# Attention with v stationary, two heads side by side, probabilities scaled on GpSimd before their transposes, and one ring of weight slots

## The chip, the cores and the metric

One core of a Trainium2 chip runs the kernel. The metric is device time in microseconds, the median of the runs. Inside a core five engines run at once and meet through semaphores: TensorE (PE; its weight loads are PEld), VectorE (DVE), ScalarE (ACT), GpSimd (POOL) and the queue of SyncE (SP), which issues DMAs.

## What is computed

One layer of a decoder trunk on 256 tokens of width 1024, 16 heads of 64. All is float32. With 256 tokens the block-sparse attention has only the causal block of its own:

```
y = rmsnorm(x, norm_mix)
q, k, v = split(y @ w_in, 3)              # 1024 x 3072
s = q @ k.T * 64**-0.5 + rel_bias[bucket(t - s)]   # causal, per head
h = x + (softmax(s) @ v) @ w_out          # 1024 x 1024
h = h + square(relu(rmsnorm(h, norm_mlp) @ w_up)) @ w_down   # 1024 x 4096, 4096 x 1024
out = rmsnorm(h, final_norm)
```

## The kernel before

Tokens lie in two blocks of 128 (`tb`). Every weight tile is 1 MB: 256 columns of an input matrix, or 256 rows of an output matrix. It lands in one of four slots of `raw`. ScalarE casts each half of it to a high part `w_hi` (`hi`, L490), VectorE subtracts it from `raw` to get a low part `w_lo` (`lo`, L668), and TensorE multiplies with both, so that three short products make one float32 product. Activations are split in the same way.

**Units.** A chunk `c` (of four) of attention is four heads: a tile of v, one of q, one of k. A v unit (L267 to L269) makes 128 tokens x 256 columns of v in 24 matmuls of 256 columns. A q or k unit (L287, L288) makes two heads' 128 features for all tokens in 8 matmuls of 512 columns and 8 of 256. Units write to banks 0 and 1 by turns. ScalarE takes out a part (`v_copy`, `qk_part`), VectorE the rest (`qk_sum`), and only then is the bank free.

**Attention of four heads `a`,** in two pairs `p`, heads `s` = 0 to 3:

- `scores` (L297, L299): per head a 128-column and a 256-column matmul over 64 rows; the two heads of a pair lie in the two halves of the array's rows. A float32 matmul is two passes, and two instructions in the profile.
- `add_bias` (VectorE, L740) adds the bias table and takes the row maximum; `softmax_exp` (ScalarE, L537) makes the exponentials in `probs` and their row sums.
- `probs_T` (L306): three transposes a head into the head's score bank; `pT_copy` (L747) brings them to `pT`.
- `values` (L320 to L322): `pT` is stationary, 64 columns of v stream: three matmuls a head, all into the bank `PV`.
- `sum_inverse` (L751) makes `rinv`, one over the row sums, and `out_rows_` (L756) multiplies the output rows by it.
- `out_T` (L330) transposes them, two a pair, and `out_hi` (L544), `out_lo` (L763) split them into `oT`.

**Order.** Each engine's order is written out by hand. In a loop over `c` = 1 to 3 TensorE puts the attention of chunk `c` - 1 between the units of chunk `c`:

```
scores(0) v(0) scores(1) v(1) probs_T(0) q(0) values(0) probs_T(1) q(1) values(1) out_T(0) k(0) out_T(1) k(1)
```

Behind the loop (L449 on) come the scores of the last four heads, the product with `w_out` in steps `mix(tb, k)` (L338), one pair's 128 features each, with the last attention between them, then the second norm (L249 transposes its rows) and the MLP in 16 steps. VectorE and ScalarE have lists of their own, in which the halves of weight tiles (`lo_in`, `hi_in`) stand between the attention steps. The q, k and v tiles use slots 0 to 2 and the fourth slot holds a `w_out` tile from the start; SyncE loads a tile as soon as `lo_done` says that the last one of its slot is converted. GpSimd only issues DMAs: the small tables, a bias table of 512 KB for each four heads (`tiles`, L225), and the gains of the norms.

Of the kernel before, what the change touches and what calls it, by code (L numbers as in the profile page):

```python
# [31 lines left out]
P = 128  # L32
# [17 lines left out]
UNITS = 6  # L50
# [25 lines left out]
def build(nc, x, rel_bias, norm_mix, norm_mlp, mlp_up, mlp_down, w_in, w_out, final_norm,  # L76
# [9 lines left out]
    with ExitStack() as ctx:  # L86
# [17 lines left out]
        v_sb = sb("v_sb", [P, TB, D])  # L104
# [3 lines left out]
        o_sb = sb("o_sb", [P, 2, TB, P])  # L108
# [24 lines left out]
        PV, OTB = 6, 7  # L133
# [13 lines left out]
        raw_free, scores_seen = sem("raw_free"), sem("scores_seen")  # L147
# [6 lines left out]
        scores_done, biased, exp_done = sem("scores_done"), sem("biased"), sem("exp_done")  # L154
        pt_done, pt_ready = sem("pt_done"), sem("pt_ready")
        rinv_done, pv_done, o_ready = sem("rinv_done"), sem("pv_done"), sem("o_ready")
        ot_done, othi_done, ot_ready = sem("ot_done"), sem("othi_done"), sem("ot_ready")
# [14 lines left out]

        @block.sync
        def _(sp):
            def load(slot, src, split):

                if split is not None:
                    sp.wait_ge(lo_done, split)
                    sp.sem_inc(raw_free, 1)
# [11 lines left out]
            load(1, w_in_v[:, :, 0:CW], None)  # L191
            load(2, w_in_v[:, :, D:D + CW], None)
            load(3, w_out_v[:, 6:8, :], None)
            with sp.Fori(1, CHUNKS_IN) as c:
                for slot, base in enumerate((2 * D, 0, D)):
                    load(slot, w_in_v[:, :, bass.ds(c * CW + base, CW)], 6 * c - 4 + 2 * slot)
            for q in range(3):
                load(q, w_out_v[:, 2 * q:2 * q + 2, :], 2 * (OUT0 + q - 3 + 1))
# [14 lines left out]
        def _(pool):  # L213
# [17 lines left out]
            with pool.Fori(1, CHUNKS_IN) as a:  # L231
                pool.wait_ge(biased, 4 * a)
                tiles(a)
# [5 lines left out]
        def _(pe):  # L239
# [13 lines left out]
            def v_unit(c, tb, first):  # L253

                if not first:
                    pe.wait_ge(lo_done, 6 * c + 2)
                    pe.wait_ge(qk_ready, 4 * c - 1 + tb)
                wh, wl = cols(w_hi, 0), cols(w_lo, 0)
# [13 lines left out]
            def qk_unit(c, u):  # L272

                slot = u // 2
                pe.wait_ge(lo_done, 6 * c + 2 * slot + 2)
                if u < 4:
                    pe.wait_ge(v_ready, 2 * c + u - 1)
                else:
                    pe.wait_ge(qk_ready, 4 * c + u - 3)
                feature_unit(bank[UNIT[u % 2]], slot, u % 2).then_inc(unit_done, 1)  # L280
# [11 lines left out]
            def scores(a, p):  # L292

                pe.wait_ge(qk_ready, 4 * a + 3 + p)
                heads = [(bank[SCORE[2 * p + h]], slice(h * DH, (h + 1) * DH)) for h in range(2)]
                for dst, dims in heads:
                    mm(dst[:, 0:P], qT[dims, p, P:T], kT[dims, p, 0:P], start=True, stop=True)  # L297
                for dst, dims in heads:
                    mm(dst[:, P:3 * P], qT[dims, p, 0:P], kT[dims, p, :], start=True, stop=True  # L299
                       ).then_inc(scores_done, 1)  # L300

            def probs_T(a, p):
                for h in range(2):
                    pe.wait_ge(exp_done, 4 * a + 2 * p + h + 1)
                    for b in range(3):
                        last = nc.tensor.transpose(bank[SCORE[2 * p + h]][:, b * P:(b + 1) * P],  # L306
                                                   probs[:, 2 * p + h, b * P:(b + 1) * P], ident[:])
                    last.then_inc(pt_done, 1)

            def values(a, p):  # L310

                if p == 1:
# [606 lines left out]
```

## Time and profile before

| | |
|---|---|
| runs | 324.13, 324.78, 325.31 us |
| median | 324.78 us |
| profiled execution, first to last instruction | 323.0 us |
| TensorE busy | 309.5 us, 96% |
| VectorE busy | 205.7 us, 64% |
| ScalarE busy | 160.9 us, 50% |
| GpSimd busy | 6.5 us, 2% |

The profiled execution has no time of its own beside its span; the median of the runs is 1.8 us above that span, which is what lies around the first and last instruction. Busy times of TensorE overlap, since its matmuls are pipelined, so what a step costs is read from one start to the next. The loop runs from 32.86 to 103.16 us, three turns of 23.43 or 23.44 us; the MLP's steps run from 142 to 317 us.

### The profile page before, as it was taken

How to read it: one execution, taken by the hardware profiler on the slowest of the kernel's cores; microseconds unless marked ns; L12 is line 12 of the kernel's file. 1: busy time of each engine (PE TensorE's matmuls, PEld its weight loads, DVE VectorE, ACT ScalarE, POOL GpSimd, SP SyncE). 2: the span in 40 equal slices, each digit the busy share in tenths (PEclk: the TensorE clock that was granted, in tenths of full speed). 3: DMA queues.
4: the chain of work that ended last, by engine and by line, in shares of the span. 5: the costliest groups of instructions: out<-in, count | busy, mean ns of one | idle time of the engine just before them, and what ended most of it. 6: DMA issues, size and time to landing. Idle time of an engine off the chain costs nothing.

```text
span 323.0 us, 5025 instructions
## 1 busy us (share of the span) xinstructions
PE 309.5 (96%) x1734; PEld 261.9 (81%) x1734; DVE 205.7 (64%) x366; ACT 160.9 (50%) x293; POOL 6.5 (2%) x14
## 2 busy tenths in 40 slices
PE   5699999999999999989999999999999999999992
PEld 2588898998997888988888888888888888888881
DVE  3786665665756657968755854675485567548454
ACT  2684734834833836535643544464455446434322
POOL 2001000000000000000000000000000000000000
PEclk9999999999999999999999999999999999999999
DMA  6989764463454373554756557465745656430003
GB/s 204 363 300 336 254 195 130 130 195 131 152 185 125 124 260 90 185 169 145 223 166 205 187 148 242 153 214 152 222 167 162 228 165 223 132 130 0 0 2 130
DMA packets 36589, 55.90 MB, mean 173 GB/s; under 512 B 1073, under 2 KB 29905, under 8 KB 36578
## 3 DMA queue, kind: packets, MB, share of 16 engines
q1 hardware_dynamic: 35586, 52.50, 49.9%
q0 software_dynamic: 992, 3.25, 3.6%
q8 instruction: 7, 0.11, 0.2%
q14 instruction: 4, 0.03, 0.0%
HBM read 54.67 MB, written 1.07 MB: 173 GB/s over the span
## 4 chain that ended last, share of the span: by engine, by line
PE 89%; DVE 4%; ACT 3%; DMA 2%; issue 1%; SPq 0%; DVEq 0%; ACTq 0%
PE bank L338 32%; PE bank L287 27%; PE bank L288 14%; PE bank L267 3%; PE bank L268 2%; PE bank L269 2%; DMA raw<-in_a_w_in_dram 2%; DVE w_lo L668 2%; PE bank L376 1%; PE bank L306 1%; PE bank L377 1%; PE bank L321 1%; PE bank L322 1%; PE bank L299 1%; PE bank L320 1%; PE bank L297 1%
## 5 line engine op out<-in xcount | busy, mean ns | idle before, releaser
L668 DVE TENSOR_TENSOR w_lo<-raw,w_hi 128x1024 fp32r<-128x1024 f32 x96 | 115.6, 1222 | 64.9 <-ACT w_hi L490 61.8
L287 PE MATMUL bank<-yT,w_hi 128*128 128x512 f32 x368 | 131.6, 399 | 0.0
L490 ACT CAST w_hi<-raw 128x1024 fp32r<-128x1024 f32 x95 | 97.6, 1048 | 56.0 <-PE bank L338 55.1
L288 PE MATMUL bank<-yT,w_lo 128*128 128x256 f32 x368 | 103.3, 281 | 0.0
L287 PEld LDWEIGHTS bank<-yT,w_hi 128*128 128x128 f32 x368 | 69.1, 188 | 16.7 <-DVE w_lo L668 0.6
L338 PE MATMUL bank<-w_hi,hT 128*128 128x512 f32 x256 | 73.3, 396 | 0.0
L288 PEld LDWEIGHTS bank<-yT,w_lo 128*128 128x128 f32 x368 | 69.5, 189 | 0.6
L338 PEld LDWEIGHTS bank<-w_hi,hT 128*128 128x128 f32 x256 | 47.1, 188 | 11.0
L338 PE MATMUL bank<-w_lo,hT 128*128 128x512 f32 x128 | 41.0, 397 | 0.0
L338 PEld LDWEIGHTS bank<-w_lo,hT 128*128 128x128 f32 x128 | 24.1, 188 | 5.9
L528 ACT ACTIVATE part<-bank 128x256 f32<-128x256 f32 x16 | 6.2, 385 | 33.0 <-PE bank L288 33.0
L551 ACT COPY part<-bank 128x256 f32<-128x256 f32 x30 | 11.2, 372 | 22.9 <-PE bank L288 22.9
L267 PE MATMUL bank<-w_hi,yT 128*128 128x256 f32 x64 | 19.5, 305 | 2.7 <-DVE yT L720 2.3
L338 PE MATMUL bank<-w_hi,oT 128*128 128x512 f32 x64 | 19.3, 399 | 0.0
L268 PE MATMUL bank<-w_lo,yT 128*128 128x256 f32 x64 | 18.6, 291 | 0.0
L269 PE MATMUL bank<-w_hi,yT 128*128 128x256 f32 x64 | 18.6, 291 | 0.0
L537 ACT ACTIVATE probs<-probs,negmax 128x128 f32<-128x128 f32 (+1 forms) x32 | 14.2, 445 | 6.1 <-DVE negmax L740 6.1
L557 ACT CAST hT<-s_sb 128x256 fp32r<-128x256 f32 x32 | 13.0, 407 | 8.2 <-DVE s_sb L782 8.2
L267 PEld LDWEIGHTS bank<-w_hi,yT 128*128 128x128 f32 x64 | 12.7, 198 | 5.4 <-DVE yT L720 2.7
L777 DVE TENSOR_TENSOR z_sb<-bank,part 128x256 f32<-128x256 f32 x30 | 12.6, 421 | 4.2 <-ACT part L551 4.2
L787 DVE TENSOR_TENSOR hT<-s_sb,hT 128x256 fp32r<-128x256 f32 x32 | 13.4, 419 | 1.9 <-ACT hT L557 1.9
L782 DVE SCALAR_TENSOR_TENSOR s_sb<-z_sb 128x256 f32<-128x256 f32 x32 | 13.6, 425 | 1.1
(73 smaller groups left out, 261.3 us busy)
## 6 DMA issues: line engine op xcount, KB each, us to landing
raw<-in_mlp_up_dram SPq DMA_DIRECT2D x16, 1024.0 KB, 5.5
raw<-in_mlp_down_dram SPq DMA_DIRECT2D x16, 1024.0 KB, 4.7
raw<-in_a_w_in_dram SPq DMA_DIRECT2D x11, 1024.0 KB, 6.7
raw<-in_a_w_out_dram SPq DMA_DIRECT2D x4, 1024.0 KB, 5.7
bias_sb<-bias_by_distance POOLq DMA_DIRECT2D x4, 512.0 KB, 5.2
h_sb<-in_x_dram SPq DMA_DIRECT2D x2, 512.0 KB, 5.2
raw<-in_a_w_in_dram SPq DMA_DIRECT2D x2, 512.0 KB, 7.2
out_dram<-y_sb SPq DMA_DIRECT2D x4, 256.0 KB, 2.2
```

What stands on the lines that cost most here:

```text
L267: mm(acc, yT[:, k, HI, tok], wh[:, k, :], start=(k == 0), stop=False)
L268: mm(acc, yT[:, k, HI, tok], wl[:, k, :], start=False, stop=False)
L269: last = mm(acc, yT[:, k, LO, tok], wh[:, k, :], start=False, stop=(k == KB - 1))
L287: mm(dst[:], wh[:, k, own], yT[:, k, :, :], start=(k == 0), stop=False, skip_group_check=True)
L288: last = mm(dst[:, 0:T], wl[:, k, own], yT[:, k, HI, :], start=False, stop=(k == KB - 1), skip_group_check=True)
L338: last = mm(bank[ACC[tb][c]][:], lhs(l), w[:, r, c * 512:(c + 1) * 512], start=first, stop=(stop and l == LO))
L490: nc.scalar.copy(w_hi[:, slot, part_of], raw[:, slot, part_of]).then_inc(hi_done, 1)
L537: last = nc.scalar.activation(probs[:, s, own], probs[:, s, own], ACT.Exp, bias=negmax[:, p, 2 * tb + h:2 * tb + h + 1], scale=-1.0, accum ...
L557: nc.scalar.copy(hT[:, par, i, HI, :], s_sb[:, i, :]).then_inc(hhi_done, 1)
L668: v.tensor_tensor(w_lo[:, slot, own], raw[:, slot, own], f32(w_hi[:, slot, own]), ALU.subtract).then_inc(lo_done, 1)
L782: v.scalar_tensor_tensor(s_sb[:, i, :], z_sb[:, i, :], 0.0, z_sb[:, i, :], ALU.max, ALU.mult).then_inc(s_done, 1)
L787: v.tensor_tensor(hT[:, par, i, LO, :], s_sb[:, i, :], f32(hT[:, par, i, HI, :]), ALU.subtract).then_inc(hT_ready, 1)
```

## The change

**TensorE.** `values` now has v stationary and streams `pT`: per head a matmul of 256 columns with the first token block's v and one of 128 columns with the second's. The output comes out as 64 features x tokens, the second head of a pair in partitions 64 to 127 of the same bank (`VALUES[p]`), which is the layout of `oT`. So `out_T`, `out_rows_` and `o_sb` go. The order of key blocks in `pT` is reversed (`(2 - b) * P`). All four heads' values are one block, and so are all four heads' scores.

**Scaling.** `probs` is multiplied by `rinv` on GpSimd (`normalise`), two instructions a head, before `probs_T`, which now waits for `normed` instead of `exp_done`.

**Order.** The units of a chunk come as q, k, v. `scores(c)` stands at the end of turn `c`; that of chunk 0 stands behind the first q unit of turn 1. Behind the loop three mixes of the second token block, not two, come before `mix_last(0)`.

**Weights.** Tiles are numbered through (`IN_PARTS`, then four of `w_out`) and use slot `t % 4`. A turn converts tiles 3c + 3 to 3c + 5; tile 5 is converted ahead of the loop and only one `w_out` tile behind it, not two. Loops over `c` are unrolled, and `v_sb` holds one chunk.

```diff
+IN_PARTS = [(0, "v"), (0, "q"), (0, "k")] + [(c, part) for c in range(1, CHUNKS_IN) for part in "qkv"]
...
-        PV, OTB = 6, 7
+        VALUES = [6, 7]
...
+            for t, (c, part) in enumerate(IN_PARTS):
+                if t:
+                    own = slice(PART_BASE[part] + c * CW, PART_BASE[part] + (c + 1) * CW)
+                    load(t % SLOTS, w_in_v[:, :, own], 2 * (t - SLOTS) + 2 if t >= SLOTS else None)
+            for q in range(CHUNKS_OUT):
+                load(q, w_out_v[:, 2 * q:2 * q + 2, :], 2 * (OUT0 + q - SLOTS) + 2)
...
+            def normalise(a, s):
+
+                p, h = s // 2, s % 2
+                pool.wait_ge(rinv_done, 2 * a + p + 1)
+                for tb, own in ((0, slice(0, P)), (1, slice(P, 3 * P))):
+                    last = nc.gpsimd.tensor_scalar(probs[:, s, own], probs[:, s, own],
+                                                   rinv[:, p, 2 * tb + h:2 * tb + h + 1], None, ALU.mult)
+                last.then_inc(normed, 1)
+
+            for a in range(CHUNKS_IN):
+                for s in range(4):
+                    normalise(a, s)
+                if a + 1 < CHUNKS_IN:
+                    pool.wait_ge(biased, 4 * a + 4)
+                    tiles(a + 1)
...
-                    pe.wait_ge(exp_done, 4 * a + 2 * p + h + 1)
+                    pe.wait_ge(normed, 4 * a + 2 * p + h + 1)
...
+            def values(a):
+
+                pe.wait_ge(v_ready, 2 * a + 2)
+                if a:
+                    pe.wait_ge(ot_ready, 2 * a)
+                for p in range(2):
+                    pe.wait_ge(pt_ready, 4 * a + 2 * p + 2)
+                    heads = [(bank[VALUES[p]][h * DH:(h + 1) * DH, :], 2 * p + h,
+                              slice((2 * p + h) * DH, (2 * p + h + 1) * DH)) for h in range(2)]
+                    for dst, s, own in heads:
+                        mm(dst[:, 0:T], v_sb[:, 0, own], pT[:, s, P:3 * P], start=True, stop=False)
+                    for dst, s, own in heads:
+                        last = mm(dst[:, 0:P], v_sb[:, 1, own], pT[:, s, 0:P], start=False, stop=True)
+                    last.then_inc(pv_done, 1)
...
+            for c in range(1, CHUNKS_IN):
+                a = c - 1
+                qk_unit(c, "q", 0)
+                if c == 1:
+                    scores(0)
+                qk_unit(c, "q", 1)
+                probs_T(a, 0)
+                qk_unit(c, "k", 0)
+                probs_T(a, 1)
+                qk_unit(c, "k", 1)
+                values(a)
+                v_unit(c, 0)
+                v_unit(c, 1)
+                scores(c)
...
             for k in range(4):
                 mix(0, k)
             probs_T(a, 0)
+            mix(0, 4)
             probs_T(a, 1)
-            mix(0, 4)
-            values(a, 0)
             mix(0, 5)
-            values(a, 1)
-            out_T(a, 0)
+            pe.wait_ge(pt_ready, 4 * a + 2)
             mix(1, 0)
-            out_T(a, 1)
+            values(a)
             mix(1, 1)
+            mix(1, 2)
             mix_last(0)
-            for k in range(2, PAIRS - 2):
+            for k in range(3, PAIRS - 2):
                 mix(1, k)
...
+            for c in range(1, CHUNKS_IN):
+                a, t = c - 1, 3 * c + 3
                 softmax_exp(a, 0)
                 softmax_exp(a, 1)
+                hi_tile(t, 0)
+                qk_part(c, "q", 0)
                 softmax_exp(a, 2)
                 softmax_exp(a, 3)
+                hi_tile(t, 1)
+                qk_part(c, "q", 1)
...
                 add_bias(a, 0)
                 add_bias(a, 1)
+                lo_tile(t, 0)
                 sum_inverse(a, 0)
                 add_bias(a, 2)
                 add_bias(a, 3)
+                qk_sum(c, "q", 0)
+                lo_tile(t, 1)
+                sum_inverse(a, 1)
+                qk_sum(c, "q", 1)
                 pT_copy(a, 0)
                 pT_copy(a, 1)
+                lo_tile(t + 1, 0)
```

On TensorE, the values of a pair and what follows them in the loop, before:

```order
L320 MATMUL bank<-v_sb,pT 128x64
L321 MATMUL bank<-v_sb,pT 128x64
L322 ISA
L322 MATMUL bank<-v_sb,pT 128x64
L320 ISA
L320 MATMUL bank<-v_sb,pT 128x64
L321 MATMUL bank<-v_sb,pT 128x64
L322 ISA
L322 MATMUL bank<-v_sb,pT 128x64
L330 MATMUL bank<-ident,o_sb 128x128 x2
```

and now, both pairs, with the end of the k unit ahead and the v unit's first matmuls behind:

```order
L310 MATMUL bank<-yT,w_lo 128x256
L344 MATMUL bank<-pT,v_sb 64x256 x2
L346 MATMUL bank<-pT,v_sb 64x128 x2
L344 MATMUL bank<-pT,v_sb 64x256 x2
L346 MATMUL bank<-pT,v_sb 64x128 x2
L292 MATMUL bank<-w_hi,yT 128x256
L293 MATMUL bank<-w_lo,yT 128x256
```

Six matmuls a pair have become four, of 64 output partitions, and the transposes of `o_sb` are gone.

On VectorE, from behind the last bias of four heads to the copies of the second pair's transposes, in the loop now (L679 is `lo`, L761 `sum_inverse`, L740 `qk_sum`, L757 `pT_copy`):

```order
L740 SCALAR_TENSOR_TENSOR qT<-bank,part 128x256 [waits part_done]
L679 TENSOR_TENSOR w_lo<-raw,w_hi 128x1024 [waits hi_done]
L761 RECIPROCAL rinv<-rowsum 128x4 [waits exp_done]
L740 SCALAR_TENSOR_TENSOR qT<-bank,part 128x256 [waits part_done]
L757 COPY pT<-bank 128x384 [waits pt_done] x2
L679 TENSOR_TENSOR w_lo<-raw,w_hi 128x1024 [waits hi_done]
L740 SCALAR_TENSOR_TENSOR kT<-bank,part 128x256 [waits part_done]
L757 COPY pT<-bank 128x384 [waits pt_done] x2
```

The second `sum_inverse` stands behind a weight conversion, as before; what is new is that the second pair's transposes wait for it.

On GpSimd, which computed nothing before, between the DMA of a gain and that of the next bias table (L237 is `normalise`):

```order
L229 DMA gain<-in_norm_mlp_dram 128x1024 [waits y_done]
L237 ISA
L237 TENSOR_SCALAR probs<-probs,rinv 128x128 [waits rinv_done]
L237 TENSOR_SCALAR probs<-probs,rinv 128x256
L237 TENSOR_SCALAR probs<-probs,rinv 128x128 [waits rinv_done]
L237 TENSOR_SCALAR probs<-probs,rinv 128x256
```

Eight such instructions now stand ahead of each bias table's DMA.

## Rows read from the trace of the kernel before

**Rows 1.** The page: the span, and TensorE's busy time, share and instructions.

```profile
span 323.0 us, 5025 instructions
...
PE 309.5 (96%) x1734; PEld 261.9 (81%) x1734; DVE 205.7 (64%) x366; ACT 160.9 (50%) x293; POOL 6.5 (2%) x14
```

**Rows 2.** The page: the chain that ended last, shares by engine.

```profile
PE 89%; DVE 4%; ACT 3%; DMA 2%; issue 1%; SPq 0%; DVEq 0%; ACTq 0%
```

**Rows 3.** Timeline of TensorE, second turn: start us, length us, what, count.

```profile
56.22 0.49 PE L297 MATMUL bank<-kT,qT 64*128 64x128 f32 x4
...
57.08 0.39 PE L267 MATMUL bank<-w_hi,yT 128*128 128x256 f32 x1
...
60.15 0.49 PE L297 MATMUL bank<-kT,qT 64*128 64x128 f32 x4
...
63.98 0.82 PE L306 MATMUL bank<-ident,probs 128*128 128x128 f32 x6
64.55 0.48 PE L287 MATMUL bank<-yT,w_hi 128*128 128x512 f32 x1
...
67.46 0.33 PE L320 MATMUL bank<-v_sb,pT 128*128 x2
...
68.74 0.83 PE L306 MATMUL bank<-ident,probs 128*128 128x128 f32 x6
...
73.47 0.39 PE L330 MATMUL bank<-ident,o_sb 128*128 128x128 f32 x2
73.61 0.48 PE L287 MATMUL bank<-yT,w_hi 128*128 128x512 f32 x1
...
79.66 0.49 PE L297 MATMUL bank<-kT,qT 64*128 64x128 f32 x4
```

**Rows 4.** 0.02 us windows of L299 alone: length, busy and instructions in flight.

```profile
56.54:56.56 0.02, 0.01 (x2) 0.02 (x4) 1.00 0.00 0
...
56.76:56.78 0.02, 0.02 (x4) 0.00 (x0) 1.00 0.00 0
```

**Rows 5.** Timeline of TensorE behind the loop, to the norm's transposes.

```profile
104.95 0.74 PE L338 MATMUL bank<-w_hi,oT 128*128 128x512 f32 x2
...
107.35 1.07 PE L338 MATMUL bank<-w_hi,oT 128*128 128x512 f32 x4
...
108.71 1.07 PE L338 MATMUL bank<-w_hi,oT 128*128 128x512 f32 x4
...
129.44 1.03 PE L249 MATMUL bank<-ident,y_sb 128*128 128x128 f32 x8
```

**Rows 6.** Timeline of VectorE: the scaling of the norm's first rows.

```profile
127.92 0.88 DVE L703 TENSOR_SCALAR y_sb<-y_sb,stat 128x512 f32<-128x512 f32 x2
```

**Rows 7.** Timelines of ScalarE (three rows) and VectorE behind the loop.

```profile
104.87 0.40 ACT L537 ACTIVATE probs<-probs,negmax 128x128 f32<-128x128 f32 x1 [1.29 <-DVE negmax L740]
...
105.76 1.03 ACT L490 CAST w_hi<-raw 128x1024 fp32r<-128x1024 f32 x1
106.70 0.40 ACT L537 ACTIVATE probs<-probs,negmax 128x128 f32<-128x128 f32 x1
...
104.19 0.29 DVE L740 CUSTOM_DVE_ANT_0 probs<-bank,bias_sb 128x128 f32<-128x128 f32 x1 [0.15 <-PE bank L299]
...
106.83 1.23 DVE L668 TENSOR_TENSOR w_lo<-raw,w_hi 128x1024 fp32r<-128x1024 f32 x1 [1.44 <-ACT w_hi L490]
107.97 0.17 DVE L751 RECIPROCAL rinv<-rowsum 128x4 f32<-128x4 f32 x1
```

**Rows 8.** Groups of VectorE's instructions by shape: busy us, mean ns, idle before.

```profile
L747 DVE COPY pT<-bank 128x384 f32<-128x384 f32 x16 | 8.0, 549 | 2.2 <-PE bank L306 2.2
...
L740 DVE CUSTOM_DVE_ANT_0 probs<-bank,bias_sb 128x256 f32<-128x256 f32 x16 | 6.7, 420 | 0.0
...
L740 DVE CUSTOM_DVE_ANT_0 probs<-bank,bias_sb 128x128 f32<-128x128 f32 x16 | 4.6, 287 | 4.4 <-PE bank L299 2.8 <-DMA bias_sb<-bias_by_distance 1.5
...
L703 DVE TENSOR_SCALAR y_sb<-y_sb,stat 128x512 f32<-128x512 f32 x8 | 3.5, 485 | 0.4
```

More of the change, by code:

```diff
@@ L290, in feature_unit, with scores @@
                 return last
[L292 to L300, printed above, removed]
+            def scores(a):
+                for p in range(2):
+                    pe.wait_ge(qk_ready, 4 * a + 3 + p)
+                    heads = [(bank[SCORE[2 * p + h]], slice(h * DH, (h + 1) * DH)) for h in range(2)]
+                    for dst, dims in heads:
+                        mm(dst[:, 0:P], qT[dims, p, P:T], kT[dims, p, 0:P], start=True, stop=True)
+                    for dst, dims in heads:
+                        mm(dst[:, P:3 * P], qT[dims, p, 0:P], kT[dims, p, :], start=True, stop=True
+                           ).then_inc(scores_done, 1)
@@ L419, in _ @@
             mm(bank[BIAS][0:HEADS, 0:BV], rel_sb[:], onehot_sb[:], start=True, stop=True).then_inc(bias_summed, 1)
-            for u in range(2, UNITS):
-                qk_unit(0, u)
-            with pe.Fori(1, CHUNKS_IN) as c:
-                scores(c - 1, 0)
-                v_unit(c, 0, False)
-                scores(c - 1, 1)
-                v_unit(c, 1, False)
-                probs_T(c - 1, 0)
-                qk_unit(c, 2)
-                values(c - 1, 0)
-                probs_T(c - 1, 1)
-                qk_unit(c, 3)
-                values(c - 1, 1)
-                out_T(c - 1, 0)
-                qk_unit(c, 4)
-                out_T(c - 1, 1)
-                qk_unit(c, 5)
+            for part in "qk":
+                for i in range(2):
+                    qk_unit(0, part, i)
+            for c in range(1, CHUNKS_IN):
[12 more added lines that the diff above has]
+                scores(c)
             a = CHUNKS_IN - 1
-            scores(a, 0)
-            scores(a, 1)
+            pe.wait_ge(v_ready, TB * CHUNKS_IN)
             for k in range(4):
@@ L622, in _ @@
             softmax_exp(a, 3)
+            hi_tile(OUT0 + 3, 1)
             nc.scalar.preload_act_table(ACT.Sqrt)
-            for half in range(2):
-                hi(3, half, 16)
             out_hi(a, 0)
@@ L814, in _ @@
                                    ).then_inc(bias_vec, 1)
-            lo_in(0, 2, 1)
-            lo_in(1, 0, 0)
-            qk_sum(0, 2)
-            lo_in(1, 0, 1)
-            qk_sum(0, 3)
-            lo_in(1, 1, 0)
-            qk_sum(0, 4)
-            lo_in(1, 1, 1)
-            qk_sum(0, 5)
-            with dve.Fori(1, CHUNKS_IN) as c:
-                a = c - 1
+            lo_tile(2, 1)
+            lo_tile(3, 0)
+            qk_sum(0, "q", 0)
+            lo_tile(3, 1)
+            qk_sum(0, "q", 1)
+            lo_tile(4, 0)
+            qk_sum(0, "k", 0)
+            lo_tile(4, 1)
+            qk_sum(0, "k", 1)
+            lo_tile(5, 0)
+            lo_tile(5, 1)
+            for c in range(1, CHUNKS_IN):
+                a, t = c - 1, 3 * c + 3
                 add_bias(a, 0)
                 add_bias(a, 1)
-                lo_in(c, 2, 0)
+                lo_tile(t, 0)
                 sum_inverse(a, 0)
```

215 lines of the change are left out of this document (84 added, 131 removed).

## The prediction

> **What bounds the kernel now.** I read the page's busy shares first: TensorE is busy for 309.5 of 323.0 us [rows 1]. The chain that ended last says the same from the other side: 89% of it is TensorE, 4% VectorE, 3% ScalarE [rows 2]. So an edit counts by what it takes off TensorE's queue or adds as a wait in it; work on VectorE, ScalarE and GpSimd costs nothing until TensorE waits for it. Next I read one turn of the loop in TensorE's timeline [rows 3]: 56.22 to 79.66, 23.44 us without a hole. The reader should look at start times there, since durations overlap: a score pair takes 57.08 - 56.22 = 0.86 us, a v unit 3.07, a transposition of two heads 0.57, a q or k unit 2.91, the values of two heads 1.28, a transposition of o 0.14. Inside a v unit 24 matmuls stand 0.12 apart (2.88); the other 0.19 is the change of array shape to and from the 64-row scores. Of a q unit 0.09 is a slower first start behind a transpose, so 2.82 inside.
>
> **What is removed from TensorE.** The new values of a pair are two matmuls of 256 and two of 128 columns, each in two passes, with the heads in two halves of the array. That is the form of a score pair, whose heads lie in two halves of the rows: two 256-column instructions are in flight at 56.55, and two more come at 56.76 [rows 4]. So side by side works there, and a step is set by the turn-round of some 0.2 us, not by columns. The trace has no column halves; bounds are 1.28 (no gain) and about 0.6 (if 64-column weights load faster than the 128-column ones). I take the score pair's 0.86, the nearest form. Per turn of the loop:
> - values: 2 x 1.28 = 2.56 becomes 2 x 0.86 + 0.19 for the shape = 1.91; saves 0.65.
> - the two transpositions of o go: 0.14 + 0.14 and the 0.09 behind the second; 0.37.
> - four score heads in one block: one change of shape less, 0.19; one slower start less, 0.09.
> That is 1.3 a turn, 3.9 for three. Behind the loop, from 104.95 to the norm's transposes at 129.44, lie 24.49 us, of which 14 mix steps of 1.36 are 19.04 [rows 5]. The rest, 5.45, is transposes, values and what TensorE waited between them. It becomes 2 x 0.66 + 1.91 = 3.23; saves 2.2. **Removed: 6.1 us.** The norm's scaling ends at 128.80 [rows 6] while its transposes begin at 129.44; they would now be due 1.36 sooner, 128.08. But the conversions that stood ahead of that norm come a step earlier too, and only its own chain from the last mix is left, so I cost this at 0, at most 0.7.
>
> The merged ring moves two halves of weight conversion (0.94 on ScalarE, 1.14 on VectorE each [rows 7]) from behind the loop to ahead of it. Their cover is the four units of the first chunk, 11.3 us; if that were short, the first biases would slip by up to 2.3. The bias table load now stands behind four scalings on GpSimd, with half a turn to spare. Unrolled loops only mean more code to fetch. All this I cost at 0.
>
> **What is added: a wait for the scaled probabilities.** Before, 1/sum was applied to the output rows and was nobody's cover. Now GpSimd multiplies the probabilities, and only then may TensorE transpose them. The queue order matters more than the multiplication, since the second 1/sum stands on VectorE behind a conversion that waits for ScalarE. Let T0 be the end of the four scores; behind the loop the trace shows that arrangement with T0 = 104.95. From it and the steps of [rows 7] (a head's exponentials 0.89, a ScalarE conversion 0.94 to the next operation and 1.03 to its end, a VectorE conversion 1.14):
> - bias of head 0 at T0 - 0.76, exponentials 0 and 1 from -0.08 to 1.70, conversion to 2.73, VectorE's part 2.77 to 3.91, first 1/sum there.
> - bias of head 2 at 4.0, exponentials 2 and 3 from 4.68 to 6.46 (0.68 behind it, as 104.87 is behind 104.19), conversion to 7.49, VectorE's part 7.53 to 8.67, second 1/sum to 8.84.
> - GpSimd starts heads 2 and 3 at about 8.95 and needs G for each. With a hand-over of 0.1, three transposes (half of 0.57) and a slower start, k unit 1 begins at 9.4 + 2G.
> By its own work TensorE would be there at 2.92 + 2.82 + 0.57 + 2.91 + 0.57 = 9.8 in turns 2 and 3. In turn 1 the scores stand behind the first q unit, which leaves one unit less of cover: 7.0. So the waits are 2.4 + 2G in turn 1 and 2G - 0.4 in each of the others, **1.6 + 6G** in all. Queued behind that wait are k unit 1, the values, v, and the next scores, so TensorE loses all of it. The first pair (scaled by about 4.2 + 2G, due at 5.7) costs nothing of its own up to G = 0.75. Behind the loop four mixes, 5.4 us, and a fifth before the second pair cover the chain: 0.
>
> G is the number that this trace lacks: GpSimd computes nothing here. Its work is an instruction of 128x128 and one of 128x256. VectorE's 512-column multiplication by a column of scalars takes 485 ns, which scaled to 384 columns is 0.36, the lower bound; its bias operation has just these two shapes, 287 + 420 = 0.71 [rows 8]; twice that, 1.42, is the upper bound. I take 0.71, the row of the same shapes. **Added: 1.6 + 4.3 = 5.9 us. Sum: -6.1 + 5.9 = -0.2**; the two balance at G = 0.75. The profile spans 323.0 us, so 322.8; the runs' median of 324.78 stands 1.8 above the span, so 324.6. A change within 0.3% (1.0 us) can't be told from none.
>
> The rows give only VectorE as a likeness. The Trainium skill (GPSIMD Engine Reference, "Performance versus the Vector engine") calls GpSimd the wrong choice for ordinary elementwise work, about twice slower than VectorE; that speaks against this change, and taken at G = 1.42 would make the sum +4.0. The same section states 1.03 cycles an element at 1.2 GHz for light one-input bodies; an estimate from that page is 0.33 us and two dispatches, and would make the sum about -1.8. No row here shows either.
>
> **The rivals.**
> 1. GpSimd is quick, G about 0.4, or the column halves turn round faster than the row halves. At G = 0.36 the wait is 3.8 and the sum -2.3: 322.5; with values of 0.6 a pair (8 x 0.26 less) 320.4. For it: one input, dense rows. Against it: 485 ns for 512 columns is VectorE's fastest row, 420 ns for 256 its usual one. Chance 0.31.
> 2. GpSimd is slow: the wait takes the place of what was saved. Place: the second transposition of each turn. It decides from G = 0.75 and passes 1 us at G = 0.92; at 1.42 the wait is 10.1, the sum +4.0: 328.8. For it: GpSimd's shortest time for anything is unknown here. Against it: the shapes are small. Chance 0.17.
> 3. VectorE and GpSimd keep each other out. Behind the second 1/sum VectorE has an addition and two copies of 549 ns each [rows 8], then at about 10.0 a conversion with two SBUF inputs. Head 3's wide multiplication would start at 8.95 + 0.71 + 0.29 = 9.95. If the conversion is first, the multiplication waits for its end at 11.15, 1.2 later, three times: +3.6 - 0.2 = +3.4, 328.2. The converse order costs TensorE nothing. Chance 0.11, since it needs both the exclusion and the loss of a close race.
> This is what the Trainium skill (SBUF — State Buffer, "SBUF: two separate sides") would have: GpSimd and a VectorE operation with two SBUF inputs share a port pair, held by whoever starts first for a whole instruction. No run of the kernel before can show it.
> 4. The change doesn't do what it says: heads in column halves run one after the other at 0.2 a pass, 1.7 a pair and not 0.86. 8 x 0.84 = +6.7: 331.3. Against it: [rows 4]. Chance 0.04.
>
> **How the numbers follow.** My forecast, G between 0.6 and 0.9 with nothing kept out, has 0.37: 324.6, itself from 323.9 to 325.7. It is nearly all within 0.3%, but some of it combines with a quicker or slower pair: 0.29 same, 0.05 faster, 0.03 slower. Rival 1 adds 0.31 to faster, rivals 2 to 4 add 0.32 to slower; 0.36, 0.29, 0.35. The range leaves out rival 4 and the ends of 1 and 2: 321.0 to 328.6.
>
> **What would show it.** Right: the transposes of the second pair start some 0.1 us behind GpSimd's end, TensorE idle about 3.8 us in turn 1 and 1.0 in turns 2 and 3, all of it ahead of the probabilities' transposes; turns of 23.1 us and a first one some 3 us longer; values at 0.86 a pair; no new wait behind the loop. Wrong: GpSimd's starts more than 1.0 apart per head or lying behind VectorE's conversions (rivals 2, 3), less than 0.5 (rival 1), the four passes of a shape one after another (rival 4), or TensorE waiting at a q or v unit, which my chain has nowhere.

## The result and the profile after

The changed kernel takes **332.32 us**, the median of 4 runs (330.91 to 332.93), against 324.95 of the kernel before on the same chip: a ratio of 1.0225 [1.0197, 1.0252]. It is slower by 7.4 us, outside my range, where I had forecast no change. The profiled execution took 332.65 us, its span is 330.8: 7.8 more than that of [rows 1].

The page of the changed kernel, its first part, the granted clock, the chain's shares and three groups:

```profile
span 330.8 us, 4655 instructions
...
PE 308.2 (93%) x1686; PEld 256.8 (78%) x1686; DVE 201.4 (61%) x358; ACT 160.0 (48%) x293; POOL 33.9 (10%) x46
...
PEclk9999969999999999999999999999999999999999
...
PE 80%; DVE 5%; POOL 5%; ACT 5%; DMA 2%; issue 1%; SPq 0%; DVEq 0%; ACTq 0%
...
L330 PE MATMUL bank<-ident,probs 128*128 128x128 f32 x48 | 8.8, 298 | 10.5 <-POOL probs L237 10.2
```

TensorE has 48 matmuls less and is hardly less busy; its share of the chain fell from 89% [rows 2] to 80%. What took its place is GpSimd (5%), and ScalarE and VectorE in front of it. The last row names the place: the transposes of the probabilities (L330) wait 10.2 us, in the whole program, for the multiplications of L237. I had added 5.9.

The timeline of TensorE in the second turn, which answers to [rows 3]; in brackets what ended an idle time before the row:

```profile
61.43 0.49 PE L320 MATMUL bank<-kT,qT 64*128 64x128 f32 x4
...
62.19 0.39 PE L320 MATMUL bank<-kT,qT 64*128 64x128 f32 x4
62.41 0.60 PE L322 MATMUL bank<-kT,qT 64*128 64x256 f32 x4
62.94 0.50 PE L309 MATMUL bank<-yT,w_hi 128*128 128x512 f32 x1
...
68.99 0.55 PE L330 MATMUL bank<-ident,probs 128*128 128x128 f32 x3
70.47 0.55 PE L330 MATMUL bank<-ident,probs 128*128 128x128 f32 x3 [0.93 <-POOL probs L237]
...
75.83 0.55 PE L330 MATMUL bank<-ident,probs 128*128 128x128 f32 x3 [1.59 <-POOL probs L237]
76.13 0.48 PE L309 MATMUL bank<-yT,w_hi 128*128 128x512 f32 x1
...
79.13 0.65 PE L344 MATMUL bank<-pT,v_sb 128*64 128x256 f32 x4
79.61 0.39 PE L346 MATMUL bank<-pT,v_sb 128*64 128x128 f32 x4
79.83 0.60 PE L344 MATMUL bank<-pT,v_sb 128*64 128x256 f32 x4
80.26 0.39 PE L346 MATMUL bank<-pT,v_sb 128*64 128x128 f32 x4
80.58 0.39 PE L292 MATMUL bank<-w_hi,yT 128*128 128x256 f32 x1
...
86.52 0.49 PE L320 MATMUL bank<-kT,qT 64*128 64x128 f32 x4
```

T0, where the scores end, is 62.94 here. k unit 1 starts at 76.13, T0 + 13.19; I had 10.82. The rows show two waits ahead of it, one in each pair, and I had one, of 1.0. A third, ahead of the first head, shows no idle time; it is 0.28 us by comparison with e1 below. The two pairs' values take 80.58 - 79.13 = 1.45 us, 0.70 and 0.75, where I had 1.91. The two pairs of scores in one block take 62.94 - 61.43 = 1.51, 0.76 and 0.75.

GpSimd in the same turn, and the two VectorE rows that bear on it:

```profile
67.42 2.99 POOL L237 TENSOR_SCALAR probs<-probs,rinv 128x128 f32<-128x128 f32 x4 [16.76 <-DVE rinv L761]
72.13 3.65 POOL L237 TENSOR_SCALAR probs<-probs,rinv 128x128 f32<-128x128 f32 x4 [1.71 <-DVE rinv L761]
```

```profile
71.86 0.17 DVE L761 RECIPROCAL rinv<-rowsum 128x4 f32<-128x4 f32 x1
...
73.19 1.22 DVE L679 TENSOR_TENSOR w_lo<-raw,w_hi 128x1024 fp32r<-128x1024 f32 x1
```

The first pair takes 2.99 us, 1.49 a head. The second takes 3.65, and a conversion with two SBUF inputs runs on VectorE in the middle of it.

The chain that ended last, through the same stretch (start, length, what), shows that nothing but this sets k unit 1:

```profile
66.01 1.23 DVE w_lo L679
...
69.75 0.94 ACT w_hi L503
...
70.72 1.23 DVE w_lo L679
71.95 0.10 DVE rinv L761
...
72.13 3.66 POOL probs L237 x4
...
75.83 0.55 PE bank L330 x3
```

It is my chain of [rows 7], step for step, with another number for its last step.

Turn 1 has one thing more. Windows of all engines (length, busy time of TensorE, its loads, VectorE, ScalarE, GpSimd, then the granted clock):

```profile
40.00:43.00 3.00, 0.16 (x2) 0.00 (x0) 2.74 (x11) 1.37 (x7) 1.44 (x2) 1.00 0.36 123
43.00:45.00 2.00, 0.95 (x5) 0.71 (x6) 0.15 (x1) 2.00 (x8) 1.55 (x3) 0.66 0.02 4
45.00:50.40 5.40, 5.40 (x19) 4.63 (x18) 3.53 (x6) 1.97 (x3) 4.15 (x5) 0.50 0.56 190
```

TensorE idles for 2.97 us before the first transposes at 43.12 and for 0.93 before those at 44.60, and the clock falls between 43 and 45 (0.66 on average) and stays at 0.50, that is 1.2 GHz, through the whole of k unit 0: 5.27 us (45.16 to 50.43) where a unit takes 2.82 inside. So there were two candidates for the loss, the multiplications' length and the clock.

Where the 7.8 us lie, by the ends of the scores: turn 1 with all that stands before it +4.87 (62.94, where the kernel before has 104.95 less two turns, 58.07; forecast +2.5), turns 2 and 3 +1.65 and +1.61, 25.09 and 25.05 against 23.44 (forecast -0.3 each), behind the loop 24.24 against 24.49, -0.25 (forecast -2.2), all else -0.1.

### The profile page after: what moved, and what is told of

Read it like the earlier page. It is cut to its first block, busy times and chain, and to the rows that moved or that the text cites. A ratio compares the mean times of both kernels' runs of the same rounds, so it can differ in the third digit from the quotient of the medians.

```text
span 330.8 us, 4655 instructions
## 1 busy us (share of the span) xinstructions
PE 308.2 (93%) x1686; PEld 256.8 (78%) x1686; DVE 201.4 (61%) x358; ACT 160.0 (48%) x293; POOL 33.9 (10%) x46
## 4 chain that ended last, share of the span: by engine, by line
PE 80%; DVE 5%; POOL 5%; ACT 5%; DMA 2%; issue 1%; SPq 0%; DVEq 0%; ACTq 0%
PE bank L354 32%; PE bank L309 22%; PE bank L310 11%; POOL probs L237 5%; ACT probs L550 3%; DVE w_lo L679 3%; PE bank L292 3%; PE bank L293 2%; PE bank L294 2%; DMA raw<-in_a_w_in_dram 2%; ACT w_hi L503 2%; PE bank L392 1%; PE bank L344 1%; PE bank L393 1%; DVE probs L750 1%
## 5 line engine op out<-in xcount | busy, mean ns | idle before, releaser
L679 DVE TENSOR_TENSOR w_lo<-raw,w_hi 128x1024 fp32r<-128x1024 f32 x96 | 115.7, 1223 | 77.3 <-ACT w_hi L503 75.0
L309 PE MATMUL bank<-yT,w_hi 128*128 128x512 f32 x368 | 133.6, 404 | 0.0
L309 PEld LDWEIGHTS bank<-yT,w_hi 128*128 128x128 f32 x368 | 70.2, 191 | 18.3 <-issue 1.0
L310 PEld LDWEIGHTS bank<-yT,w_lo 128*128 128x128 f32 x368 | 70.7, 192 | 0.6
L237 POOL TENSOR_SCALAR probs<-probs,rinv 128x128 f32<-128x128 f32 (+1 forms) x32 | 27.3, 867 | 65.2 <-DVE rinv L761 65.2
L330 PE MATMUL bank<-ident,probs 128*128 128x128 f32 x48 | 8.8, 298 | 10.5 <-POOL probs L237 10.2
L541 ACT ACTIVATE part<-bank 128x256 f32<-128x256 f32 x16 | 6.1, 382 | 24.7 <-PE bank L310 24.5
L750 DVE CUSTOM_DVE_ANT_0 probs<-bank,bias_sb 128x128 f32<-128x128 f32 (+1 forms) x32 | 9.4, 351 | 12.0 <-PE bank L322 11.9
L330 PEld LDWEIGHTS bank<-ident,probs 128*128 128x128 f32 x48 | 5.4, 147 | 14.2 <-POOL probs L237 13.9
```

The lines of the kernel that those rows point to most:

```text
L237: last = nc.gpsimd.tensor_scalar(probs[:, s, own], probs[:, s, own], rinv[:, p, 2 * tb + h:2 * tb + h + 1], None, ALU.mult)
L309: mm(dst[:], wh[:, k, own], yT[:, k, :, :], start=(k == 0), stop=False, skip_group_check=True)
L310: last = mm(dst[:, 0:T], wl[:, k, own], yT[:, k, HI, :], start=False, stop=(k == KB - 1), skip_group_check=True)
L330: last = nc.tensor.transpose(bank[SCORE[2 * p + h]][:, (2 - b) * P:(3 - b) * P], probs[:, 2 * p + h, b * P:(b + 1) * P], ident[:])
L679: v.tensor_tensor(w_lo[:, slot, own], raw[:, slot, own], f32(w_hi[:, slot, own]), ALU.subtract).then_inc(lo_done, 1)
```

## The experiments

Edits are against the changed kernel unless said otherwise. The kernel before stood at 325.34 us beside the first four, 325.06 beside the next four, 325.32 beside the last two. The profiled executions differ in the start-up too: TensorE waits there from 1.21 us (e1) to 2.95 us (e4) for the first `yT`, 1.87 in the change. So a difference of under 1 us between two totals is not read below; the lengths of turns are.

### e1: no multiplication at all

```diff
-                for s in range(4):
-                    normalise(a, s)
...
-                    pe.wait_ge(normed, 4 * a + 2 * p + h + 1)
+                    pe.wait_ge(exp_done, 4 * a + 2 * p + h + 1)
```

> Leaves the scaling by 1/sum out, so the output is that of unscaled probabilities; TensorE's transposes wait for the exponentials alone. Theory A (the time was lost in the wait for scaled probabilities, of which GpSimd's multiplications are the larger part): with 1/sum and the multiplications off the chain the second pair is ready at about T0 + 6.6, ahead of its turn at 9.8, all waits of turns 2 and 3 go, turn 1 keeps about 0.5; turns 2 and 3 fall from 25.07 to about 21.8 us, and the time to about 318 (before less 6.1 and a further 1.2, since values measure 0.70 a pair and not 0.86). Theory B (the new order of units, the ring or the column halves cost what was lost): it stays above 325.

Measured: 320.65 us (319.61 to 321.59), a ratio of 0.9874 [0.9838, 0.9910]; span 318.4. Turns 2 and 3 take 21.7 us each by the starts of the next scores, and from the end of the last scores (102.64) to the norm's transposes (124.93) are 22.29 us. TensorE's timeline, those places and the one wait left in the turns:

```profile
42.41 0.76 PE L307 MATMUL bank<-yT,w_hi 128*128 128x512 f32 x1 [2.26 <-DVE qT L738]
...
57.74 0.49 PE L318 MATMUL bank<-kT,qT 64*128 64x128 f32 x4
...
79.42 0.49 PE L318 MATMUL bank<-kT,qT 64*128 64x128 f32 x4
...
101.13 0.49 PE L318 MATMUL bank<-kT,qT 64*128 64x128 f32 x4
...
102.64 0.74 PE L352 MATMUL bank<-w_hi,oT 128*128 128x512 f32 x2
...
124.93 1.04 PE L260 MATMUL bank<-ident,y_sb 128*128 128x128 f32 x8
```

So the multiplications and their waits cost 332.32 - 320.65 = 11.7 us in all, and the rest of the change gains 4.7. I had expected 318; turns 2 and 3 came as expected, turn 1 did not. Behind the loop the gain is exactly the 2.2 of the forecast (24.49 - 22.29), so what ate it was the wait. And turn 1 has a wait of its own that the scaling hid: k unit 0 waits 2.26 us for `qk_sum` of q, whose bank it needs, since VectorE's queue has a weight conversion that waits for ScalarE (39.53) and the biases of heads 2 and 3 ahead of it (it starts at 41.84). Between 42.40 and 45.70 the granted clock is 0.50 again.

### e2: the multiplications on VectorE

```diff
+            def normalise_v(a, p):
+                dve.wait_ge(rinv_done, 2 * a + p + 1)
...
+                        last = v.tensor_scalar(probs[:, s, own], probs[:, s, own],
+                                               rinv[:, p, 2 * tb + h:2 * tb + h + 1], None, ALU.mult)
...
                 add_bias(a, 3)
+                normalise_v(a, 0)
...
                 sum_inverse(a, 1)
+                normalise_v(a, 1)
```

> The same multiplications on VectorE, behind the same 1/sum. Theory A: about 0.5 us a head by the 485 ns row, so k unit 1 starts at about T0 + 10.4 and not T0 + 13.2; waits of 0.6 in turns 2 and 3, 3.4 in turn 1: about 322.5 to 324. Theory B: no change from 332. Theory C (the place of the second 1/sum, behind a weight conversion, is the cost and not who multiplies): saves less than a third of the 7.4 us lost, about 330.

Measured: 323.72 us (321.29 to 324.86, 10 runs), 0.9950 [0.9926, 0.9974]. Against the change on GpSimd that is 8.6 us less, with the same work, the same order on TensorE and the same waits in the program. Turns 2 and 3 take 22.5 us, 0.8 more than in e1. Nearly all of that is the first pair, whose multiplications stand behind the biases of heads 2 and 3 on VectorE (66.41): from its transposes to the next unit it takes 1.10 us (67.01 to 68.11) and in e1 0.57, and it starts 0.23 later. The one long wait left is that of turn 1, for the first pair as well:

```profile
43.50 1.59 PE L328 MATMUL bank<-ident,probs 128*128 128x128 f32 x6 [2.90 <-DVE probs L766]
...
67.01 1.23 PE L328 MATMUL bank<-ident,probs 128*128 128x128 f32 x6
```

### e3: the second 1/sum ahead of the conversion

```diff
                 qk_sum(c, "q", 0)
-                lo_tile(t, 1)
                 sum_inverse(a, 1)
+                lo_tile(t, 1)
```

> GpSimd scales as in the change, but the second 1/sum stands ahead of the weight conversion in VectorE's list. Theory A: 1/sum comes at about T0 + 6.9 and not 8.9, but GpSimd is busy with the first pair to T0 + 7.5, so the second pair ends at about 10.6, or 11.2 if VectorE's conversion holds it up; 1.6 to 2.2 us saved a turn: 326 to 327.5. Theory C: the full 2.0 us a turn and the order alone brings the time to 325 or below. Theory B: no change.

Measured: 331.26 us (330.38 to 331.92), 1.0198 [1.0166, 1.0230]: about 1 us gained, 0.6 in each of turns 2 and 3, where I had expected 1.6 to 2.2 a turn. In turn 2 the second 1/sum is ready at 69.35 instead of 71.86, but GpSimd still has the first pair in hand, and its row shows all eight in one piece:

```profile
66.99 7.71 POOL L237 TENSOR_SCALAR probs<-probs,rinv 128x128 f32<-128x128 f32 x8 [16.94 <-DVE rinv L761]
```

So once 1/sum is early, GpSimd's own queue is the bound: 7.71 us, where four heads at 1.49 would be 5.96; two conversions lie inside. My expectation had one conversion in it, and of a smaller cost.

### e4: TensorE kept busy in turn 1

```diff
                 qk_unit(c, "q", 1)
+                if c == 1:
+                    pe.wait_ge(lo_done, unit_of(1, "k") + 2)
+                    for j in range(12):
+                        mm(bank[7][:], cols(w_hi, 0)[:, j % KB, 0:P], yT[:, j % KB, :, :], start=True, stop=True)
                 probs_T(a, 0)
```

> Twelve matmuls into an unused bank fill TensorE's idle 2.97 us of turn 1; the output is unchanged. In the change the k unit behind that gap runs at the lower clock, 5.27 us and not 2.82. Theory D (the clock in turn 1 costs what it seems to, 2.5 us): 329.6. Theory A (GpSimd is the bound there as well, and ends only 0.5 us before that slow unit does): 0.6 to 0.8 us less, 331.6, with the wait moved behind the k unit.

Measured: 332.67 us (331.5 to 332.83), 1.0230 [1.0199, 1.0260]: no gain. The clock stays at 1.00 and k unit 0 has its usual length, but the wait comes back behind it, at the second pair:

```profile
40.62 2.91 PE L448 MATMUL bank<-yT,w_hi 128*128 128x512 f32 x12
43.80 0.55 PE L330 MATMUL bank<-ident,probs 128*128 128x128 f32 x3 [0.27 <-POOL probs L237]
45.28 0.55 PE L330 MATMUL bank<-ident,probs 128*128 128x128 f32 x3 [0.94 <-POOL probs L237]
...
50.64 0.55 PE L330 MATMUL bank<-ident,probs 128*128 128x128 f32 x3 [1.59 <-POOL probs L237]
```

Turn 1 is 0.76 us shorter than in the change (25.11 against 25.87), as theory A had it, and its start is 0.67 later (scores end at 37.74 against 37.07, behind the longer wait in the start-up), which hides that in the total. So the half clock cost 0.8 us here, not its 2.45: for the rest TensorE would have waited for GpSimd anyway. k unit 1 is due at T0 + 13.19 by GpSimd alone, in turn 1 as in turn 2.

### e5 and e6: one unit more of cover, on GpSimd and on VectorE

```diff
                 qk_unit(c, "q", 1)
-                probs_T(a, 0)
                 qk_unit(c, "k", 0)
-                probs_T(a, 1)
+                probs_T(a, 0)
                 qk_unit(c, "k", 1)
-                values(a)
+                probs_T(a, 1)
                 v_unit(c, 0)
+                values(a)
                 v_unit(c, 1)
```

With it `sum_inverse(a, 1)` goes ahead of the conversion `lo_tile(t, 1)`, `qk_sum(c, "k", 0)` ahead of the transposes' copies, and in turn 1 the q units' addends go ahead of the second exponentials and biases. e6 is the same with the multiplications on VectorE.

> GpSimd scales as in the change; the transposes of each pair stand one unit later in TensorE's order, and the second 1/sum ahead of the weight conversion. Theory A (the multiplications cost only because too few units lie between scores and transposes): the pairs are ready at about T0 + 7.6 and T0 + 11, due at 8.6 and 12.0 in turns 2 and 3 (no wait) and at 5.7 and 9.2 in turn 1 (some 2 us): turns 2 and 3 of 21.8 us, 320 to 321. Theory E (GpSimd's work beside VectorE slows VectorE or the ring, wherever it stands): turns stay above 23.4, 324 or more.

> The same order with the multiplications on VectorE. Theory A: no wait in turns 2 and 3, at most 0.5 in turn 1 and no fall of the clock there: 318 to 319. If VectorE's own load becomes the bound (4 us more in each turn of 21.8), the waits move to the q and k units: 321 or more.

Measured: e5 321.34 us (320.27 to 321.75), 0.9872 [0.9853, 0.9891]; e6 320.01 us (318.98 to 321.7), 0.9841 [0.9825, 0.9858]. Both are above what I had expected, by 0.3 and 1.0 us, while turns 2 and 3 take 21.9 in both, as expected. In e5 GpSimd is as slow as ever, but under cover; TensorE waits for it in turn 1 alone within the turns (0.24 and 0.93). GpSimd's timeline of e5, the first turn and behind the loop (6.51 and 6.50 in the turns between):

```profile
42.45 6.48 POOL L237 TENSOR_SCALAR probs<-probs,rinv 128x128 f32<-128x128 f32 x8 [13.30 <-DVE rinv L764]
...
104.57 7.44 POOL L237 TENSOR_SCALAR probs<-probs,rinv 128x128 f32<-128x128 f32 x8 [12.57 <-DVE rinv L764]
```

Behind the loop, where e5 has the change's order, 24.26 us stay as they were in the change (102.16 to 126.42); e6 takes 22.27 there (103.73 to 126.00). In e6's profile turn 1 lost time of its own, TensorE's timeline:

```profile
49.33 0.36 PE L290 MATMUL bank<-w_hi,yT 128*128 128x256 f32 x1 [1.83 <-DVE kT L741]
```

v unit 0 waits for k's `qk_sum`, and from 50.00 to 53.30 the granted clock is 0.50. Not every execution of e6 has this: the mean granted clock is 0.989 and 0.988 in two of its six (321.70, the profiled one, and 321.67 us) and 0.994 to 0.999 in the other four (318.98 to 320.03).

### e7: one multiplication a head

```diff
-                for tb, own in ((0, slice(0, P)), (1, slice(P, 3 * P))):
+                for tb, own in ((1, slice(0, 3 * P)),):
```

> One multiplication of 128x384 a head instead of 128x128 and 128x256; the first 128 columns get the other token block's factor. If an instruction costs GpSimd a fixed 0.58 us and 1.5 ns a column (from the means 771 and 963 ns), a head takes about 1.15 us and not 1.5, and 0.7 us a turn are saved: 330. If the cost goes by columns alone, a head stays at 1.4 to 1.5 and the time at 332.

Measured: 329.29 us (one run), span 327.5. The list of GpSimd's instructions by source line, of the change and then of e7 (min, median and max ns):

```profile
L237 POOL TENSOR_SCALAR probs<-probs,rinv x32: 593/912/1649, 41.6 to 122.0; 128x128 f32<-128x128 f32 x16, 128x256 f32<-128x256 f32 x16
```

```profile
L237 POOL TENSOR_SCALAR probs<-probs,rinv x16: 1233/1244/2167, 41.3 to 118.0; 128x384 f32<-128x384 f32 x16
```

593, 912 and 1244 ns for 128, 256 and 384 columns are 2.5 ns a column and some 0.27 us fixed (593 is the shortest 128-column one; the median falls on a 256-column one that nothing stretched). My expectation took the means of the page, which held instructions stretched by a conversion, and so made a column cheaper and the fixed part larger than they are. A head is 1.24 instead of 1.49 us. The second pair is stretched here too, to 3.39 where two would take 2.48. So it is only 0.26 shorter than in the change, and turns 2 and 3 are shorter by as little (24.84 against 25.07), not by the 0.7 that I had expected. The total is near my 330 for other reasons: behind the loop 22.66 us against 24.24, turn 1 24.83 against 25.87.

### e8: values head by head

```diff
                     for dst, s, own in heads:
                         mm(dst[:, 0:T], v_sb[:, 0, own], pT[:, s, P:3 * P], start=True, stop=False)
-                    for dst, s, own in heads:
                         last = mm(dst[:, 0:P], v_sb[:, 1, own], pT[:, s, 0:P], start=False, stop=True)
```

> The values' matmuls of a pair in the order head by head, so that two instructions in different column halves do not follow each other as 256, 256, 128, 128 but as 256, 128, 256, 128. If column halves overlap as the rows' do, the pair needs four steps and more and goes from 0.70 to about 1.1 us, 3 us in all at most, of which the waits hide none. If the halves never overlapped, the pair stays at 0.70.

Measured: 333.12 us (one run), 0.5 above the change's profiled 332.65. That is no more than the start-up, which is 0.7 longer here. The miss is mine: a pair still takes 0.70 us (79.46 to 80.16), so the order of the heads does not matter there. It is not my second branch either, by which the halves never overlapped. TensorE's timeline of e8:

```profile
79.46 0.66 PE L344 MATMUL bank<-pT,v_sb 128*64 128x256 f32 x4
79.94 0.40 PE L345 MATMUL bank<-pT,v_sb 128*64 128x128 f32 x4
```

The wide passes of both heads still start ahead of any narrow one, though in the program head 0's narrow ones stand before head 1's wide ones. So the two heads run side by side.

### e9: e6 with k's addend ahead in turn 1

```diff
                 softmax_exp(a, 3)
+                if c == 1:
+                    qk_part(c, "k", 0)
                 hi_tile(t, 1)
...
+                if c == 1:
+                    qk_sum(c, "k", 0)
                 lo_tile(t, 1)
```

> The kernel with the later transposes and VectorE's multiplications waits once in turn 1, 1.83 us at the v unit, since ScalarE takes out the k unit's part behind three weight conversions; the clock falls behind that wait. Here that part comes first in turn 1. If the wait is ScalarE's order, it goes with the fall of the clock: 2.5 to 3 us less than that kernel, 317 to 318. If VectorE's load is the bound, the wait only moves: above 319.5.

Measured: **319.43 us** (318.12 to 319.56, 5 runs), 0.9799 [0.9779, 0.9818], the fastest here, though not the 317 to 318 that I had expected. Its page, the span and the clock, and then the one wait left on TensorE in the turns:

```profile
span 317.7 us, 4654 instructions
...
PEclk9999999999999999999999999999999999999999
```

```profile
53.10 0.36 PE L290 MATMUL bank<-w_hi,yT 128*128 128x256 f32 x1 [0.69 <-DVE kT L744]
```

No stretch of half clock is left, and behind the loop it takes 22.28 us (101.58 to 123.86), the 2.2 less that the change had promised. So e6's wait of 1.83 and the clock behind it came from k's addend standing in the queues behind conversions; the multiplications are the same in both. But part of the wait moved instead of going: it is now v unit 1 that waits, for k's second addition, which stands on VectorE behind copies and conversions and starts at 52.52. By the ratios e9 gains 1.4 us on e6; the two profiled spans differ by 2.2, but most executions of e6 had no fall of the clock.

### e10: a conversion moved off the second pair

```diff
                 pT_copy(a, 1)
-                lo_tile(t + 1, 0)
                 qk_sum(c, "k", 0)
                 pT_copy(a, 2)
                 pT_copy(a, 3)
+                lo_tile(t + 1, 0)
```

> The change, with VectorE's weight conversion that follows the first two copies moved behind all four. Theory F (a VectorE operation with two SBUF inputs and a GpSimd multiplication keep each other out): GpSimd's second pair takes 3.0 us as the first does and not 3.65, and k unit 1 starts 0.65 us sooner in each turn: 330.4, the span near 329. Theory G (the second pair is slow for another reason, such as ScalarE's casts or the DMAs): it still takes 3.65 and the time stays at 332.

Measured: 331.28 us (330.37 to 331.55), 1.0176 [1.0158, 1.0195], about 1 us less than the change, 1.6 by the ratios to the kernel before. Turns 2 and 3 take 24.5 us, 0.6 less each. GpSimd's timeline of e10, second turn, and TensorE's behind it:

```profile
71.77 2.99 POOL L237 TENSOR_SCALAR probs<-probs,rinv 128x128 f32<-128x128 f32 x4 [1.71 <-DVE rinv L761]
```

```profile
74.82 0.55 PE L330 MATMUL bank<-ident,probs 128*128 128x128 f32 x3 [0.94 <-POOL probs L237]
```

With nothing else changed on GpSimd the second pair falls from 3.65 to 2.99 us, that of the first, and TensorE's wait from 1.59 to 0.94. So the conversion had kept a multiplication out for 0.66 us. The Trainium skill (SBUF — State Buffer, "SBUF: two separate sides"), by which GpSimd and a VectorE operation with two SBUF inputs hold a shared port pair in turn, agrees with these rows in that the multiplication is held out. The rows do not show that whoever starts first keeps the other out for a whole instruction: in the change the conversion starts at 73.19, while GpSimd's multiplication of 72.71 (0.93 long, to 73.64) is still recorded as running, and both have their usual length; it is the next multiplication that is stretched. The copies and additions of VectorE that also lie beside the pair, and read at most one operand from SBUF, stretch nothing: 2.99 with them as for the first pair, whose second head is multiplied while VectorE is idle.

## Why the prediction was wrong

**The step that failed is G.** I wrote "I take 0.71, the row of the same shapes". GpSimd takes 1.49 us a head. My upper bound was "twice that, 1.42", so even the bound was short, by 0.07. With two G in each chain that alone is 2.99 - 1.42 = +1.57 a turn. The likeness with VectorE was the fault: VectorE does these four multiplications in 1.00 us (e6, 42.17), 0.5 a pair of shapes, below the row of 0.71, and GpSimd in 2.99, three times as long. The row that I called nearest erred in both directions, because it was another operation on another engine. The Trainium skill (GPSIMD Engine Reference, "Performance versus the Vector engine") said about twice slower, measured there on an addition of two inputs; the factor measured here is 3, in the direction it warned of. Its 1.03 cycles an element, from which I had the estimate of 0.33 us a head, is not what these rows show, and the -1.8 that I gave with it needs 0.45 a head: no row shows the 0.12 for two dispatches in that.

**Rivals 2 and 3 came together.** I had priced them apart, the one at 328.8, the other at 328.2. The exclusion happened in each of the three turns (3.65 instead of 2.99), and not where I placed it: a slow GpSimd is still at work when the conversion comes, so no close race was needed. That my chances treated them as two small cases was the second error: the first makes the second nearly certain.

**The sum of a turn, redone.** k unit 1 came at T0 + 13.19, 2.37 later than the 10.82 of the forecast: +1.57 from G, +0.66 from the exclusion, +0.24 from the later start behind the second 1/sum (T0 + 9.19 against 8.95), less 0.1 of hand-over. Against that the values took 1.45 where I had 1.91, 0.46 less. Together 1.9, which is the miss of turns 2 and 3 (1.63 + 0.3). The 0.46 has a cause that the rows of before could have told: the score pair's 0.86 stood alone and held the change of shape at both its ends, and I added 0.19 for the shape once more. Nor is a step some 0.2 us whatever its columns, as I wrote: it is 0.11 for the two heads' passes of 128 columns (62.19 to 62.41 holds two such steps) and 0.22 for those of 256 (79.83 to 80.26), in row halves as in column halves. The wait there is 25.07 - 21.7 = 3.4 us a turn by e1, of which the trace shows 0.93 + 1.59 as idle. The rest lies in rows that count as busy: the first transposes stand at T0 + 6.05 and in e1 at T0 + 5.77, 0.28 later; the first pair takes 1.79 us (68.99 to 70.78) and in e1 0.57, 0.29 more than its idle time explains, and the second 2.44 (73.69 to 76.13), 0.28 more.

**The first pair, "scaled by about 4.2 + 2G, due at 5.7",** would cost nothing up to G = 0.75, I wrote. It was scaled at T0 + 7.5 and its wait of 0.93 is that; but since the second pair's end alone sets k unit 1, it adds nothing to the loss of a turn.

**Turn 1.** The miss of 2.4 is the same 2.37, plus 0.8 of half clock (e4), less the values' 0.46 and less 0.3 that I did not trace. I had no term for the clock. I had also written of TensorE waiting at a q or v unit "which my chain has nowhere". For a k unit it was there all along under the scaling: e1 laid open 2.26 us behind `qk_sum` of q. The chain had only the transposes' wait in it, and missed that VectorE's additions stand in the same queue behind the same conversion and biases. TensorE's idle time in turn 1, 2.97 + 0.93 = 3.9, is near my 3.8 by luck: I had placed it ahead of the second pair, and it stands ahead of the first.

**Behind the loop.** "four mixes, 5.4 us, and a fifth before the second pair cover the chain: 0" was wrong by 1.95 us. TensorE's timeline of the change there:

```profile
121.51 0.55 PE L330 MATMUL bank<-ident,probs 128*128 128x128 f32 x3 [0.30 <-POOL probs L237]
122.99 0.55 PE L330 MATMUL bank<-ident,probs 128*128 128x128 f32 x3 [0.93 <-POOL probs L237]
```

GpSimd works from 115.49 for 7.44 us in one piece and ends at 122.93, and the last transposes follow at 122.99. The mix behind them starts at T0 + 10.21 and in e1 at T0 + 8.24 (110.88), 1.97 earlier. At G = 0.71 this would have been covered by my estimate: e7 shows GpSimd waiting there for the second 1/sum until T0 + 5.48, and 1.42 more is 6.9, ahead of the 8.0 at which e1 transposes the last head. So it is the same failed term again, with conversions inside.

**What was right:** 6.1 us removed (e1's turns of 21.7 are 0.4 better than the 22.14 of the forecast, its tail is the 2.2 to the digit, by luck: transposes and values take 0.57 + 0.57 + 1.45 = 2.59 there where I had 3.23, and the other 0.64 went into steps that I did not trace), the time of each 1/sum to 0.3 us, the waits in turns 2 and 3 standing ahead of the probabilities' transposes alone, the break-even as such: with VectorE's 0.5 in it my sum is -6.1 + 1.6 + 3.0 = -1.5, and e2 measured 1.6 us less than before (though there the half clock of turn 1 and the quicker values, which I had not in it, set off each other, so the agreement is in part luck). The merged ring and the norm showed no cost of their own.

**What to do with it.** e9 is faster than both kernels. It has the column halves and the order with more cover, and no work on GpSimd; no run takes the column halves away from it. e5 shows that GpSimd can do it almost as well where it is covered (0.9872 against 0.9841, the difference of 1.3 us less than the 2.0 that its tail alone loses). Open stays whether e5 with e9's turn 1 and a tail with more cover would reach e9, whether k's second addition put further ahead would take away the 0.69 us left in turn 1, and what the column halves alone bring; none was tried.

## What to carry to other kernels

Work moved to an engine that computed nothing before has no price in the old trace. Measure it alone, or look whether the change survives a price well above the nearest row, before counting its gain: here it was 2.1 times that row, and 3 times the same work on VectorE. And a wait for slow work is best answered by distance: one unit more between the scores and their transposes, with the VectorE queue put in the same order, gained 11 us (e5) with the slow multiplications still in place. How much of the 11 is the distance alone is not told apart: e5 also has the second 1/sum ahead of the conversion, which by itself gained 1 us (e3), and the additions reordered.

## What the runs showed of the hardware that I had not expected

- A GpSimd multiplication of fp32 by a column of scalars takes 593, 912 and 1244 ns at 128, 256 and 384 columns; VectorE's takes 299 and 347 ns as means at the first two (e6).
- A multiplication on GpSimd beside a VectorE conversion with two SBUF inputs is held up by 0.66 us (3.65 against 2.99, e10), by 0.5 to 0.9 elsewhere (e5 6.48 against 5.96; e3 7.71, two conversions; e7 3.39 against 2.48).
- The clock fell to 0.50 after idle times of TensorE of 1.83 us (e6, in two executions of six by their mean clock) and 2.26 us (e1), for 3.3 us each, and for over 6 us with 2.97 and 0.93 close together (the change). After the 0.69 us of e9 it did not, nor after the 0.93 and 1.59 us of turns 2 and 3.
- Two heads in column halves take 0.70 us for their eight passes, in either order of the heads (e8), and 0.75 with the change of shape behind them. Two heads in row halves take 0.76 and 0.75 in a block of the same kind, so neither is the faster; the 0.86 of [rows 3] is a pair with the change of shape at both ends.
